# Feed-forward of the first layer: the norm's squares added on GpSimd, two weight slots split ahead, and the last group's first two tiles taken together

## The reference, cut to what matters

```python
h = h + rmsnorm(mix, norm_mix_post)
a = rmsnorm(h, norm_ffn_pre) @ w_ffn_in                 # 1024 -> 2 x 2816
a = sum(ap[:, j:j + L] * conv_w[j] for j in range(3)) + conv_b
val, gate = a[..., :D_FF], a[..., D_FF:]
y = (gelu(gate) * val) @ w_ffn_out                      # 2816 -> 1024
return h + rmsnorm(y, norm_ffn_post)
```

## Time and profile before

| | us |
|---|---|
| median of 3 runs (1955.08 to 1962.77) | 1958.05 |
| the profiled execution, its own time | 1958.58 |
| its span in the profile | 1956.8 |
| mixer of layer one, from the start | 0 to about 434 |
| feed-forward of layer one | about 434 to 852 |
| the second layer | about 852 to the end |

### The profile page before, as it was taken

One profiled execution on the slowest core, in us unless ns is written; L12 is line 12 of the kernel. 1 busy time (PEld: TensorE's weight loads), 2 busy tenths in 40 slices (PEclk: granted clock), 3 DMA queues, 4 the chain that ended last, 5 costly groups with the idle time before them and its releaser, 6 DMA issues. The chain is left out here.

```text
span 1956.8 us, 38581 instructions
## 1 busy us (share of the span) xinstructions
PE 1784.4 (91%) x17168; PEld 1532.5 (78%) x17168; DVE 1021.0 (52%) x1524; ACT 650.2 (33%) x1060; POOL 88.5 (5%) x115
## 2 busy tenths in 40 slices
PE   6998789978999999988999998888669999999998
PEld 5888667877998989878777777677558888878877
DVE  3246564435663654554665355655556545353554
ACT  3242233433442332343333334333144322121232
POOL 6000000010000000010000000000001100000020
PEclk8999987988999999989999999999979999999999
DMA  5211130030222222221212100000052222222221
GB/s 160 87 66 44 55 108 1 1 109 32 99 87 106 88 87 87 89 100 65 76 65 103 70 34 4 4 5 10 3 204 87 90 104 87 108 86 97 97 87 65
DMA packets 29132, 144.57 MB, mean 74 GB/s; under 512 B 6315, under 2 KB 9659, under 8 KB 14380
## 3 DMA queue, kind: packets, MB, share of 16 engines
q1 hardware_dynamic: 24828, 133.58, 19.1%
q0 software_dynamic: 3856, 7.87, 1.3%
q10 hardware_dynamic: 288, 0.73, 0.1%
HBM read 134.82 MB, written 8.91 MB: 73 GB/s over the span
## 5 line engine op out<-in xcount | busy, mean ns | idle before, releaser
L228 DVE TENSOR_TENSOR w_w_lo<-w_w_raw,w_w_hi 128x2048 fp32r<-128x2048 f32 x67 | 153.5, 2292 | 192.7 <-ACT w_w_hi L215 192.4
L240 PE MATMUL f_bank<-u_hi,w_w_hi 128*128 128x258 f32 x704 | 203.5, 289 | 12.3 <-DVE w_w_lo L228 6.2
L241 PE MATMUL f_bank<-u_hi,w_w_lo 128*128 128x258 f32 x704 | 202.3, 287 | 0.0
L242 PE MATMUL f_bank<-u_lo,w_w_hi 128*128 128x258 f32 x704 | 200.9, 285 | 0.0
L240 PE MATMUL g_bank<-g_y_hi,g_w_hi 128*128 128x512 f32 x384 | 151.1, 394 | 16.5 <-DVE g_w_lo L228 12.2
L242 PE MATMUL g_bank<-g_y_lo,g_w_hi 128*128 128x512 f32 x384 | 150.3, 391 | 0.0
L241 PE MATMUL g_bank<-g_y_hi,g_w_lo 128*128 128x512 f32 x384 | 150.2, 391 | 0.0
L240 PEld LDWEIGHTS f_bank<-u_hi,w_w_hi 128*128 128x128 f32 x704 | 135.3, 192 | 13.7 <-DVE w_w_lo L228 6.4
L215 ACT ACTIVATE g_w_hi<-g_w_raw 128x2048 fp32r<-128x2048 f32 x45 | 85.9, 1908 | 166.9 <-PE g_bank L242 165.3
L215 ACT ACTIVATE w_w_hi<-w_w_raw 128x2048 fp32r<-128x2048 f32 x67 | 127.6, 1904 | 32.0 <-PE f_bank L242 32.0
L242 PEld LDWEIGHTS f_bank<-u_lo,w_w_hi 128*128 128x128 f32 x704 | 136.1, 193 | 0.0
(11 more groups left out here) (509 smaller groups left out, 3980.0 us busy)
## 6 DMA issues: line engine op xcount, KB each, us to landing
g_w_raw<-in_w_ff SPq DMA_DIRECT2D x32, 1024.0 KB, 4.7
w_w_raw<-in_w_in SPq DMA_DIRECT2D x30, 1024.0 KB, 4.8
w_w_raw<-in_w_ffn_in SPq DMA_DIRECT2D x22, 1024.0 KB, 4.8
w_w_raw<-in_w_ffn_out SPq DMA_DIRECT2D x12, 1024.0 KB, 4.8
w_w_raw<-in_w_o SPq DMA_DIRECT2D x4, 1024.0 KB, 5.1
gate_pre<-rw_t POOLq DMA_DIRECT2D x16, 256.0 KB, 2.3
g_w_raw<-in_w_up SPq DMA_DIRECT2D x4, 1024.0 KB, 8.8
g_branch<-gate_pre SPq DMA_DIRECT2D x4, 1024.0 KB, 11.9
```

The costliest lines, as they stand in the source:

```text
L228: nc.vector.tensor_tensor(R.lo[:, r, 0:size], R.raw[:, r, 0:size], R.hi[:, r, 0:size].bitcast(F32), ALU.subtract).then_inc(R.split, 1)
L240: nc.tensor.matmul(out, w_hi, u_hi, start=start, stop=False)
L241: nc.tensor.matmul(out, w_lo, u_hi, start=False, stop=False)
L242: return nc.tensor.matmul(out, w_hi, u_lo, start=False, stop=stop)
```

## The change

Opening: GpSimd adds the squares of chunks 0 to 6 into `h_sum` (which lies in `c`, unused until then), and PE sums by token once for that total and once for chunk 7, both inside slot 2 after the first half of its first tile. ACT's next square waits for GpSimd's add, no longer for PE. Slot 2 is split (ACT and DVE) right after the first norm's root and diagonal, slot 3 after the second's; slot 3 was split in `hidden` before. ACT runs a gelu on one column ahead of `rms`. DVE makes `u_lo` of chunk 0 ahead of the add of chunk 1. Last group: PE takes five of the six rows for the first two tiles and then the last row for both; in the 22nd slot DVE splits the next weights after `y_lo` instead of before it.

```diff
+        sq_added, h_added = sem("sq_added"), sem("h_added")
+        h_sum = c[:].rearrange("p a b n -> p (a b n)")[:, 0:L]
+        warm = sb("warm", [P, 1])
@@ gpsimd
+            add_squares(pool, nc, h_sq, h_sum, h_squared, h_added)
             add_squares(pool, nc, sq, sq_sum, psquared, sq_added)
@@ tensor, first_slot
-                    pe.wait_ge(h_squared, k + 1)
-                    sum_tokens(pe, nc, C, bank[:, 3, :], h_sq[:, k % 2, :], T, TG, k == 0, k == KT - 1).then_inc(h_summed, 1)
@@ second_slot, after the 8 chunks of a half
+                        if m == 0 and half is outs[2 * r][0][0]:
+                            pe.wait_ge(h_added, KT - 1)
+                            sum_tokens(pe, nc, C, bank[:, 3, :], h_sum, T, TG, True, False)
+                            pe.wait_ge(h_squared, KT)
+                            sum_tokens(pe, nc, C, bank[:, 3, :], h_sq[:, (KT - 1) % 2, :], T, TG, False, True).then_inc(h_summed, 1)
@@ the last group's first slot of the second product
+            def paired_slot(ph, q, r, rows, first):
+
+                pe.wait_ge(R.split, 2 * q + r + 1)
+                pe.wait_ge(R.tile_free, ph.c0)
+                for ks in (range(len(rows) - 1), [len(rows) - 1]):
+                    for m in range(2):
+                        out = whole[(r * 2 + m) % len(whole)][0][0]
+                        for k in ks:
+                            pe.wait_ge(y_done, first + k + 1)
+                            at = k * SLOT + m * P
+                            last = three_pass(nc, out, R.hi[:, r, at:at + P], R.lo[:, r, at:at + P],
+                                              y_hi[:, rows[k], :], y_lo[:, rows[k], :], k == 0, k == len(rows) - 1)
+                        if k == len(rows) - 1:
+                            last.then_inc(R.tile_done, 1)
@@ scalar
+            ahead_hi(act, nc, R, into[0].n0 + 1, into[0].c0)
             for k in range(KT):
...
                 if k >= 2:
-                    act.wait_ge(h_summed, k - 1)
+                    act.wait_ge(h_added, k - 1)
                 nc.scalar.activation(h_sq[:, k % 2, :], h[:, k, :], ACT.Square).then_inc(h_squared, 1)
-                if k == 4:
-                    ahead_hi(act, nc, R, into[0].n0 + 1, into[0].c0)
-            act.wait_ge(h_summed, KT)
+            act.wait_ge(h_summed, 1)
             nc.scalar.activation(stat[0:T, 1, :], bank[0:T, 3, 0:TG], ACT.Sqrt, scale=1.0 / D, bias=EPS).then_inc(tok_std, 1)
+            ahead_hi(act, nc, R, into[0].n0 + 2, into[0].done(0))
+            nc.scalar.activation(warm[:], C("ones")[:, 0:1], ACT.Gelu_apprx_tanh)
             act.wait_ge(row_done, 2)
@@ scalar, hidden
-                hi_ahead(act, nc, R, ph, j, q, r)
+                if not (isinstance(t, int) and t == 0):
+                    hi_ahead(act, nc, R, ph, j, q, r)
@@ vector
+            ahead_lo(dve, nc, R, into[0].n0 + 1)
             dve.wait_ge(row_done, 1)
...
+                    if k == 1:
+                        remainder(0)
                     dve.wait_ge(scaled, k + 1)
...
-            ahead_lo(dve, nc, R, into[0].n0 + 1)
+            ahead_lo(dve, nc, R, into[0].n0 + 2)
@@ vector, hidden
-                lo_ahead(dve, nc, R, ph, j, q, r)
+                turned = isinstance(t, int) and t in (0, FT - 1)
+                if not turned:
+                    lo_ahead(dve, nc, R, ph, j, q, r)
...
+                if turned and t:
+                    lo_ahead(dve, nc, R, ph, j, q, r)
```

More of the change, by code:

```diff
@@ L1295, in ffn_block @@
         sq_sum = a[:, 0, 0, 0:GRID]
-        sq_added = sem("sq_added")
+        sq_added, h_added = sem("sq_added"), sem("h_added")
+        h_sum = c[:].rearrange("p a b n -> p (a b n)")[:, 0:L]
+        warm = sb("warm", [P, 1])
         part = NEAR // 2
@@ L1366, in into_slot, with out_slot @@
                     gemm_slot(pe, nc, R, into[g], j, q, r, u_hi, u_lo, outs)
+            def paired_slot(ph, q, r, rows, first):
[11 more added lines that the diff above has]
+                            last.then_inc(R.tile_done, 1)
+            def out_slot(g, j, q, r):
+                if g == 2 and isinstance(j, int) and j == 0:
+                    paired_slot(out[g], q, r, places[g], 8 * g)
+                else:
+                    gemm_slot(pe, nc, R, out[g], j, q, r, y_hi, y_lo, whole, places[g], ready=(y_done, 8 * g))
             for g, (t0, count) in enumerate(groups):
                 each_slot(pe, into[g], lambda j, q, r, g=g: into_slot(g, j, q, r))
-                each_slot(pe, out[g], lambda j, q, r, ph=out[g], rows=places[g], ready=(y_done, 8 * g):
-                          gemm_slot(pe, nc, R, ph, j, q, r, y_hi, y_lo, whole, rows, ready=ready))
+                each_slot(pe, out[g], lambda j, q, r, g=g: out_slot(g, j, q, r))
         @block.scalar
@@ L1434, in _, with remainder @@
             on_diagonal(dve, nc, C, diag, stat[0:T, 0, :], T, TG).then_inc(tok_diag, 1)
+            ahead_lo(dve, nc, R, into[0].n0 + 1)
             dve.wait_ge(row_done, 1)
             dve.wait_ge(h_back, 16)
+            def remainder(k):
+                dve.wait_ge(u_hi_done, k + 1)
+                nc.vector.scalar_tensor_tensor(u_lo[:, k, :], h[:, k, :], column("ffn_pre", k),
+                                               u_hi[:, k, :].bitcast(F32), ALU.mult, ALU.subtract).then_inc(u_done, 1)
             for k in range(KT + 1):
@@ L1440, in _ @@
                                                    ALU.mult, ALU.mult).then_inc(scaled, 1)
+                    if k == 1:
+                        remainder(0)
                     dve.wait_ge(scaled, k + 1)
                     nc.vector.tensor_tensor(h[:, k, :], h[:, k, :], acc[:, k, :], ALU.add).then_inc(added, 1)
-                if k:
-                    dve.wait_ge(u_hi_done, k)
-                    nc.vector.scalar_tensor_tensor(u_lo[:, k - 1, :], h[:, k - 1, :], column("ffn_pre", k - 1),
-                                                   u_hi[:, k - 1, :].bitcast(F32), ALU.mult, ALU.subtract).then_inc(u_done, 1)
+                if k >= 2:
+                    remainder(k - 1)
             nc.vector.memset(a[:, :, :, NEAR:NEAR + 1], 0.0).then_inc(edges, 1)
```

## The result

The changed kernel takes 1948.17 us (median of 6 runs, 1944.23 to 1953.03), the kernel before beside it 1959.83 (6 runs): ratio 0.9936, 95% interval 0.992 to 0.9952. That is faster by 11.7 us, 0.6%, where 13.7 had been forecast and 1944.3 us named. The stated range, 1939 to 1949, and the sign hold; the narrower range of pace and fits, 1942 to 1946, does not. The profiled execution has a span of 1942.5 us against 1956.8.

What follows compares the result with a forecast made beforehand. PE, busy 91% of the span, was taken as the bound, with time won at its waits and slow clock. Terms -0.8 - 4.0 - 2.7 - 1.7 + 0.2 - 4.7 = -13.7 us gave 1944.3 us, range 1939 to 1949.

Steps and rivals of the forecast that it cites:

- the narrower range of pace and fits: Whole kernel: 1942 to 1946 us, from a slot 1 pace of 2.7 to 3.2 us a chunk and the tight fits.
- What the adds cost DVE: Opening, slot 1: GpSimd's adds block DVE instructions with two SBUF inputs, nothing to 1.1 us a chunk; estimated pace 2.95.
- Slot 1, -0.8: Opening: with DVE setting the pace, PE ends slot 1 at about 462.7, 0.8 us earlier.
- Slot 2, -4.0: Opening: no wait for slot 2's remainder; end of slot 1 to second tile takes 10.1 us instead of 14.1.
- Slot 3, -2.7 and -1.7: Opening: the wait for slot 3's remainder goes, saving 2.7 us, and the slow clock behind it, saving 1.7 us.
- slot 4 +0.2: Slot 4's remainder is done 17.6 us after `rms`, while PE wants it after 17.4: 0.2 us lost.
- From slot 5 on DVE needs 10.6 us a slot against PE's 11.55: Feed-forward of layer one: DVE needs less time a slot than PE from slot 5 on.
- time saved ahead of it is kept: From slot 3 to the last group's turn other engines follow PE, so savings ahead of PE are kept and add.
- The rival of a tight fit that breaks: `rms`, slot 4's remainder, the turn's next remainder, or worse add collisions lose 2 to 5 us: 1946 to 1949; chance 0.12.
- The last group, -4.7: Last group's turn: the 3.28 us wait for `y_lo` and 1.46 us lost restarting at 1.2 GHz go.
- a slot 1 that spoils slot 2: Clock falls in gappy slot 1 and slot 2 begins slowly: some 3 us lost, 1947.3 us; chance 0.14.
- a PE that stays at 1.2 GHz: Low clock persists through slot 2, eating the gain (+1 us), or through slot 3, 1970 us; chance 0.03.

Runs made afterwards that it cites:

- the second profile: The changed kernel itself, unmodified, run and profiled once more: stage 401.21 us, median 1949.61 us, ratio 0.9948 to the kernel before.
- the experiment on its place: Changed kernel with slot 2's high part back among the chunks and its remainder right behind the last `u_lo`: stage 403.63 us, median 1947.19 us, ratio 0.9944.
- the kernel with PE's sums and the wait by bank: Changed kernel with PE summing each chunk's square in slot 1 and second-product tiles waiting only for their own bank; measured twice: 1945.04 and 1943.97 us.

## Why the prediction was right, and where it was not

**What the adds cost DVE.** Right in kind and place. The stretched rows of the second layer gave 1.1 us for an add that meets an instruction with two inputs in SBUF; here it is 1.16 (1.87 against 0.71) and 1.04 (1.80 against 0.76), and nothing for the multiply, which has one in PSUM. By the rule of the Trainium skill (SBUF — State Buffer, section SBUF: two separate sides) whoever starts first has the shared ports for the whole instruction and the other is fully blocked. The trace nearly agrees: the add ends 1.87 us after it wanted to start, where the two in turn would take 1.31 + 0.71 = 2.02. From the fourth multiply to the last a step took 3.1 us on average in the first profile (444.83 to 457.25, four steps) and 2.9 in the second; the 2.95 I chose lies between. The alternation that I had stepped through held in the second profile and broke off in the first. By the rows it hangs on who is first when both start 0.01 us apart, and so differs between executions.

**Slot 1, -0.8.** +0.4 in the first profile and -0.6 in the second.

**Slot 2, -4.0.** -4.15 measured; root, split, table load and `rms` ran in the order and the time of the forecast, and that tight fit held. The reason given, that the remainder is 20 us old, was not the one that counts: a remainder that ends together with slot 1 does as well, by the experiment on its place.

**Slot 3, -2.7 and -1.7, slot 4 +0.2.** -4.1 of -4.2 measured up to the end of group one's tiles.

**"From slot 5 on DVE needs 10.6 us a slot against PE's 11.55", "time saved ahead of it is kept".** This is the step that failed: the sum has no term for the first turn, as if DVE had time to spare all through group one. The earlier trace rows show that DVE waits for PE in slots 20 and 21, and I took that for the whole stage ("at each tile there"). In group one of before only the last of the 18 multiplies by `rms` waits for PE, 0.19 us. All the others find their tile ready: DVE starts the group behind PE, and of the 27.0 us that it is idle in the changed kernel between its first and its last multiply there, 25.5 end with an instruction of ACT and none with one of PE; so the two in turn set the pace. That pace is 10.6 us a slot in slots 3 and 8 and 11.3 to 11.5 in slots 4 to 7 (66.80 us for the six, from 492.81 to 559.61), before and after alike; why it is longer in those four stays open. Slot 3's early split takes 4.1 us off PE's way from `rms` to the turn, but off DVE's only 1.8, since one split has moved ahead of `rms` (8.85 us from slot 1's first multiply to slot 2's, against 10.62), and 0.3 more of slack. PE starts at the turn 2.1 us earlier, counted from `rms`, and waits 2.0 us more; in the first profile 1.7 us of slow clock came behind. What was saved ahead of `rms`, in slots 1 and 2, is kept whole, for DVE starts earlier by as much. The rival of a tight fit that breaks named three places, and this was not among them. That one row of before, 568.99 [0.19 <-PE], was the sign of it.

**The last group, -4.7.** -5.0 in the profile and 5.2 by undoing it.

**The clock.** It didn't fall in slot 1 in spite of gaps of 0.7 to 1.7 us, once PE was at 2.4 GHz. The rivals of a slot 1 that spoils slot 2 and of a PE that stays at 1.2 GHz have no trace here. That it would fall behind a wait at the turn, and in some executions only, was in neither sum nor rivals.

**The sum.** -9.1 us in the stage in one profile and -11.75 in the other, against -13.7. The medians' 11.7 and 11.9 us lie near the latter, but they hold the second layer's differences as well, so that nearness is in part luck. That the first profile's execution came out at 14.3 us less is owed to what lies outside the stage, the second layer above all, and no merit of the sum. One sum of the chances doesn't add up: by its own parts, 0.58, 0.13, 0.14 and half of 0.12, faster has 0.91 and not 0.86.

## What to carry to other kernels

Ask of each saving whether it comes to all engines that meet at the next place where one waits for another. What was saved ahead of `rms`, from which both PE and DVE set out, was kept whole; what PE alone saved behind it was kept only as far as its follower's way became shorter too, by the split that had moved away (1.8 us) and the little time that the follower had stood idle for PE (0.2 to 0.3 us). Whether an engine follows is read in each group of tiles and not in one stretch for all. Moving work to GpSimd takes VectorE's time where both work from SBUF: let GpSimd's instruction begin beside a VectorE instruction that reads PSUM, or leave the work on TensorE if there it costs 1 us a chunk and stands in nobody's way. A wait that covers a whole group of buffers, when only one is needed, is worth replacing before anything ahead of it is tuned: here it was worth 6.5 us of the stage to the changed kernel, of which 1.7 are the slow clock that didn't follow the wait in every execution. What slot 3 gave is then kept whole: 87.0 us from `rms` to the turn, against 92.15 before, of which 0.83 were the wait.

## What the runs showed of the hardware that I had not expected

TensorE can be busy without a gap and have a low clock. In the one profile that has them, eight sums with one column a matmul in a row, 9.94 us, saw it go from 2.4 to 1.2 GHz. The second layer's opening also has such sums between its matmuls, and there PE can be at 1.2 GHz while busy; a stretch of the kernel with PE's sums and the wait by bank (the opening's first matmul is at 843.18), and the same part of the work in the change's first profile (first matmul at 851.60):

```profile
854.00:862.00 8.00, 8.00 (x52) 8.00 (x51) 4.12 (x6) 2.49 (x4) 0.00 (x0) 0.69 0.09 40
```
```profile
862.42:870.42 8.00, 8.00 (x71) 8.00 (x71) 2.57 (x4) 3.12 (x5) 0.00 (x0) 1.00 0.11 45
```

How long this lasts is not the kernel's alone: the opening's first slot took 21.1 us in the change's first profile and 27.0 in its second, 23.2 in both of before, 26.8 to 27.0 in all four profiles of changed kernels without GpSimd's adds in the first layer, and 20.9 to 25.0 in the rest. What follows the stage differs by up to 12 us (1103.0 to 1114.6), about 6 of them in that opening and the rest in slow stretches further on; that fits with a stage shorter by 18.4 us (412.96 to 394.59) giving medians shorter by only 15 to 16.5. What decides when the clock comes up there stays open; no run here changed that opening alone.
